# Weight splits in pieces during the scan, a partial first pass over four tiles of the output projection, and a partial first pass over three tiles of the last two down groups

## The reference

```
h      = modulate(rmsnorm(x, norm1_g))                 (and the same for the context)
q, k, v, o, gates, u, vb, ga, gb = split(h @ w_in)
h_a    = bidirectional chunked mLSTM scan(q, k, v, gates)      (4 heads, chunks of 128)
y_a    = rmsnorm(h_a, head_g) * sigmoid(o)
y_b    = gelu(u) * (w_spatial @ rmsnorm(gelu(vb)) + b)
merged = sigmoid(ga) * (y_a @ w_pa) + sigmoid(gb) * (y_b @ w_pb)
x      = x + g1 * (merged @ w_out)
f      = silu(h2 @ w_ff1) * (h2 @ w_ff3)               h2 = modulate(rmsnorm(x, norm2_g))
out    = rmsnorm(x + g2 * (f @ w_ff2), final_g)
```

## Time and profile before

| | us |
|---|---|
| median of 3 runs | 1909.56 (1909.21 to 1912.38) |
| the profiled execution | 1913.69 |
| its span | 1912.0 |
| PE busy / DVE busy / ACT busy | 1833.0 / 993.7 / 553.3 |

### The profile page before, as it was taken

The page is one execution under the profiler, slowest core; times in us unless marked ns, Lnnn a source line. Parts: engine busy times, 40 slices in busy tenths (PEclk is TensorE's granted clock), DMA queues, the critical chain, the costliest instruction groups (busy, mean ns, idle before and its releaser), DMA issues.

```text
span 1912.0 us, 24057 instructions
## 1 busy us (share of the span) xinstructions
PE 1833.0 (96%) x9052; PEld 1534.2 (80%) x9052; DVE 993.7 (52%) x1571; ACT 553.3 (29%) x842; POOL 131.8 (7%) x131
## 2 busy tenths in 40 slices
PE   6898999999989999999999999999999999999987
PEld 3596797978879988888888878788888888788876
DVE  3676636556355543211221164675655566666657
ACT  5533132322312322111221131443334333311111
POOL 1001010100112000000100000000000000231200
PEclk9899999999999899999999999999999999999989
DMA  7200100202048201111411152122222232632302
GB/s 295 60 17 17 56 23 23 66 22 66 12 137 282 88 22 44 57 53 44 124 52 44 44 176 88 66 66 67 93 82 88 66 100 76 232 130 89 122 8 88
DMA packets 91337, 157.15 MB, mean 82 GB/s; under 512 B 4466, under 2 KB 73218, under 8 KB 86930
## 3 DMA queue, kind: packets, MB, share of 16 engines
q1 hardware_dynamic: 83906, 130.11, 20.3%
q0 software_dynamic: 7376, 26.28, 4.1%
HBM read 132.26 MB, written 24.12 MB: 82 GB/s over the span
## 4 chain that ended last, share of the span: by engine, by line
PE 89%; DVE 7%; issue 2%; ACT 1%; DMA 0%; DVEq 0%; SPq 0%; ACTq 0%
PE PD L1803 26%; PE PD L1818 11%; PE PD L2164 10%; PE PM L2164 10%; PE PD L2183 6%; PE PM L2183 6%; PE PD L2090 5%; PE PM L1803 5%; PE PM L2108 1%; PE PD L2108 1%; PE PM L2038 1%; PE PD L1885 1%; DVE Cst L1382 1%; PE PM L1844 1%; PE PM L1876 1%
## 5 line engine op out<-in xcount | busy, mean ns | idle before, releaser
L1803 PE MATMUL PD<-R_hi,whi 128*128 128x512 f32 x480 | 149.8, 393 | 1.7 <-DVE Hh L1405 1.7
L1803 PE MATMUL PD<-R_lo,whi 128*128 128x512 f32 x480 | 148.5, 391 | 0.0
L1803 PE MATMUL PD<-R_hi,wlo 128*128 128x512 f32 x480 | 148.1, 390 | 0.0
L1818 PE MATMUL PD<-whi,R_hi 128*128 128x256 f32 x512 | 145.0, 283 | 0.0
L1818 PE MATMUL PD<-wlo,R_hi 128*128 128x256 f32 x512 | 144.9, 283 | 0.0
L1818 PE MATMUL PD<-whi,R_lo 128*128 128x256 f32 x512 | 144.9, 283 | 0.0
L1158 DVE TENSOR_TENSOR wlo<-raw,whi 128x1024 fp32r<-128x1024 f32 x76 | 89.9, 1219 | 93.7 <-ACT whi L745 93.7
L745 ACT ACTIVATE whi<-raw 128x1024 fp32r<-128x1024 f32 x76 | 76.4, 1049 | 158.9 <-PE PD L1803 95.5
L1803 PEld LDWEIGHTS PD<-R_hi,whi 128*128 128x128 f32 x480 | 89.2, 188 | 21.4 <-issue 3.0
L1803 PEld LDWEIGHTS PD<-R_hi,wlo 128*128 128x128 f32 x480 | 90.4, 188 | 19.2
L1803 PEld LDWEIGHTS PD<-R_lo,whi 128*128 128x128 f32 x480 | 90.4, 188 | 19.1
(11 more groups left out here) (406 smaller groups left out, 4097.7 us busy)
## 6 DMA issues: line engine op xcount, KB each, us to landing
raw<-in_w_in SPq DMA_DIRECT2D x46, 512.0 KB, 4.5
rawF<-in_w_ff SPq DMA_DIRECT2D x44, 512.0 KB, 5.0
ada<-in_w_ada POOLq DMA_DIRECT2D x32, 512.0 KB, 5.9
f_dram<-Fo SPq DMA_DIRECT2D x11, 1024.0 KB, 4.8
w_raw<-in_w_ff SPq DMA_DIRECT2D x11, 1024.0 KB, 5.0
f_raw<-f_dram SPq DMA_DIRECT2D x11, 1024.0 KB, 6.9
ada_raw<-in_w_ada SPq DMA_DIRECT2D x8, 1024.0 KB, 19.8
raw<-in_w_in SPq DMA_DIRECT2D x20, 256.0 KB, 3.6
```

Of the source, the lines that this page charges most:

```text
L1803: i = mm(dst[:, e * HALF:e * HALF + width], wk[:, k, :], part, start=(k == 0 and step == 0), stop=(k == KT - 1 and step == 2))
L1818: i = mm(PD[s][:, e * HALF:e * HALF + CW], src[:, k, at], wk[:, k, :], start=(k == 0 and step == 0), stop=(k == KT - 1 and step == 2))
```

## The change

Three edits, independent of one another.

1. Scan: the two halves of `wlo[A]`, made in j=3 and j=5, become eight pieces of 256 columns, one in each step from j=2 to j=9. `w_ready[0]` is counted after the piece of j=5 and `w_ready[1]` after that of j=9.
2. Output projection: ACT splits the second block of `w_out` after seven `m_hi`, and DVE after seven `m_lo`, both ahead of the last merge; `m_hi(7)` and `m_lo(7)` follow the merge. PE does k=0 to 6 of tiles 0 and 1, waits for the second PD buffer, does k=0 to 6 of tiles 2 and 3, then k=7 of the four tiles, then tiles 4 to 7 in full.
3. Down projection: PE does group 9's part of tiles 0 to 2 when group 9's split is there, then waits for group 10's split, does its part of these tiles, and then tiles 3 to 7 in full.

```diff
@@ ACT, gates_a
                 split_next(i * 2 + (N_PA + 2), A, None)
                 if last:
-                    for k in range(KT):
+                    for k in range(KT - 1):
                         m_hi(k)
                 split_next(i * 2 + (N_PA + 3), B, i * 2 + (T_PA + 2))
+                if last:
+                    m_hi(KT - 1)
@@ DVE
+            def split_lo_piece(n, buf, piece):
+
+                half, at = piece // 4, slice(piece * CW, (piece + 1) * CW)
+                dve.wait_ge(hi_done, n * 2 + (half + 1))
+                i = v.tensor_tensor(wlo[buf][:, at], raw[half][:, piece % 4 * CW:(piece % 4 + 1) * CW],
+                                    whi[buf][:, at].bitcast(F32), ALU.subtract)
+                if piece % 4 == 3:
+                    i.then_inc(w_ready[half], 1)
@@ DVE, attend
-                    if j in (3, 5):
-                        split_lo(h * 3 + (N_H + 3), A, (j // 2 - 1,))
+                    if j >= 2:
+                        split_lo_piece(h * 3 + (N_H + 3), A, j - 2)
                     if j < CT:
                         continue
@@ DVE, merge_a
                     if m == 0:
                         split_lo(i * 2 + (N_PA + 2), A)
                         if last:
-                            for k in range(KT - 2):
+                            for k in range(KT - 1):
                                 m_lo(k)
+                            split_lo(i * 2 + (N_PA + 3), B)
                 if last:
-                    for k in range(KT - 2, KT):
-                        m_lo(k)
-                split_lo(i * 2 + (N_PA + 3), B)
+                    m_lo(KT - 1)
+                else:
+                    split_lo(i * 2 + (N_PA + 3), B)
@@ PE
-            for m in range(2):
-                free(T_O + m)
-
-            def out_tile(hf, t):
+
+            def out_tile(hf, t, ks=range(KT)):
...
-                for k in range(KT):
+                for k in ks:
...
-                last.then_inc(out_mm, 1)
+                if ks[-1] == KT - 1:
+                    last.then_inc(out_mm, 1)
...
-            for t in range(LT):
+            free(T_O)
+            for t in range(2):
+                out_tile(0, t, range(KT - 1))
+            free(T_O + 1)
+            for t in range(2, 4):
+                out_tile(0, t, range(KT - 1))
+            for t in range(4):
+                out_tile(0, t, range(KT - 1, KT))
+            for t in range(4, LT):
                 out_tile(0, t)
...
-            def down(r, t, pars, halves_last=False):
-
-                pe.wait_ge(summed, r * LT + (t + 1))
+            def down(r, t, pars, halves_last=False, opens=True, closes=True):
+
+                if opens:
+                    pe.wait_ge(summed, r * LT + (t + 1))
...
-                              start=(n == 0), stop=(n == len(steps) - 1))
+                              start=(opens and n == 0), stop=(closes and n == len(steps) - 1))
...
-                    last.then_inc(down_done, 1)
+                    if closes:
+                        last.then_inc(down_done, 1)
...
+            pe.wait_ge(down_ready, 2 * NFB - 2)
+            for t in range(3):
+                down(NFB - 2, t, (1,), closes=False)
             pe.wait_ge(down_ready, 2 * NFB)
-            for t in range(LT):
+            for t in range(3):
+                down(NFB - 2, t, (0,), opens=False)
+            for t in range(3, LT):
                 down(NFB - 2, t, (1, 0), t == LT - 1)
```

## The result

The changed kernel takes 1899.44 us (median of 10 runs, 1898.38 to 1905.35), the kernel before 1909.61 in the same comparison (10 runs, 1906.77 to 1914.03). The ratio is 0.9949 with a 95% interval of 0.9939 to 0.9958, that is 9.7 us less (8.0 to 11.6). The forecast was 1900.8 within 1897.0 to 1906.5. The profiled execution took 1902.24, its span is 1899.7.

The account below looks back on a forecast made before the run. PE was taken as the bound, busy for 1833.0 of 1912.0 us. The terms 6.2 - 5.3 - 9.7 gave -8.8 us: 1904.9 for the profiled execution, 1900.8 for the median, range 1897.0 to 1906.5.

Parts of the forecast that it names:

- DVE's pieces: Scan, heads 0 to 2: six pieces, 2.04 us, replace 2.27 us before Hh's 14th write; 0.2 us gained per head, 0.6 together.
- One sign of the forecast: Scan: the changed profile would show DVE pieces of 0.42 us and no PE wait for `Cst`.
- The late load: Last head's scan: raw[1]'s later reload delays ACT's split and squares, 6.1 us slower, plus 0.7 us of low clock.
- the 6.2 of the forecast: Whole scan edit: -0.6 + 6.1 + 0.7 = 6.2 us slower, bounds 4.4 to 8.7.
- Heads 0 to 2 are covered: Scan, heads 0 to 2: the next head's first two matmul groups hide the delay; of 14 us cover, 8 remain.
- Output projection: Before the output projection: 3.6 us less wait and 1.7 us of clock, 5.3 us faster (3.1 to 5.3), 0.7 idle left.
- The join: Output projection, tiles 3 and 4: tile 0's residual ready at 1136.9, needed at 1137.3; a miss would cost under 0.5 us.
- Down projection: Last two down groups: no wait for group 10's split; 9.7 us faster, 3.0 of it clock (bounds 9.0 to 9.7).
- The free late load: Rival, scan's last head: the late load costs nothing, -15.5 us in all, 1894.1; chance 0.08.
- The output projection gives nothing: Rival: clock falls anyway and freed time becomes waits at k=7 or tile 4; -3.5 us in all, 1906.1; chance 0.11.
- The slow load: Rival, raw[1] in each head: late load uncovers all heads, kernel slower; break-even at 11.9 us load; chance 0.04.

Follow-up runs that it names:

- pieces early: The changed kernel with its eight pieces made two per step in j=2 to j=5, raw[1] given back in j=5: 1892.52 us, ratio 0.9915.
- two late halves: The changed kernel with two halves, in j=5 and j=9, instead of eight pieces: 1900.08 us, ratio 0.9945.
- squares first: The changed kernel with ACT's split of block B moved behind the eight squares, in every head: 1894.25 us, ratio 0.9914.
- the filled pause: The changed kernel with 56 unread PE products of 512 columns before the last head's transposes: 1901.35 us, ratio 0.9946.

## Why the prediction was right

**DVE's pieces.** Six pieces at 0.34 in place of 2.27 us: the next instruction starts 0.34 after a piece, as worked out from the 512 and 1024 columns of the earlier trace rows. Counted from head 0's transposes the last pause begins 1.0 us earlier; three times 0.2 was forecast. The sum of the waits for `Cst` and `Hh` fell by 0.7 (8.5 to 7.8). One sign of the forecast did not come: it had no wait of PE for `Cst`, and 5.4 us of them are left. They were 8 of up to 1.1 us and are 16 of 0.4 at most: smaller pieces shorten each of them and spread them over the steps. It has no weight in the sum, where they were counted at nothing. The Trainium skill, "VectorE: DVE Perf Modes", section on the TRN2 errata, gives an estimate of (256+151)/0.96 = 424 ns for a piece: the trace agrees with 0.42 as the length of one. Laid end to end such pieces would have made a loss; the trace has 0.08 of each overlapped by the next instruction, so the formula is right for the length of one and too dear for a row of them.

**The late load.** From the last piece to the end of the last square 9.5 us were forecast (538.2 to 547.7) and 9.45 measured (537.29 to 546.74). By parts: end of the piece to ACT's split 3.6 us (3.7), split 0.96 to the first square (1.06), squares 4.51 (4.3, as their spacing alternates between 0.53 and 0.62). PE's wait is 14.8 instead of 14.4, as PE is there a little earlier. The clock behind it loses 2.4 us instead of 1.6; 2.3 was taken. The scan edit measured so is +5.5 and +0.7, the 6.2 of the forecast (its upper bound of 8.7 doesn't follow from its terms, 0.8 + 6.1 + 1.4 = 8.3). By times it is +3.8 (the edit alone) and +6.7 (the whole change against the change without it), and the first of these is the worst-fitting number on the scan. Heads 0 to 2 are covered: no wait for their transposes appears. What PE waits for `Hh` there (2.4 us in 3) is for the 14th write, which was so before (1.7 in 3); with the waits for `Cst` shorter, PE comes to it sooner.

**Output projection.** 3.6 us of wait and 1.7 of clock: the stage is 5.3 shorter, with 0.68 us of idle left where 0.7 was forecast, and a clock of 1.00. The join has no wait.

**Down projection.** 243.4 us from first to last product were forecast (1647.2 to 1890.6), 243.3 measured (1644.70 to 1888.03). The stage began 2.5 us earlier, and tile 0 closes at 1855.9 for 1858.4, the next 2.65 us behind it. DVE falls behind and waits for PE again at 1877.58, at tile 5 rather than tile 6.

**The sum.** -8.8 was forecast, -10.2 is the difference of the medians (-9.7 by the ratio, -8.0 to -11.6 by its interval), -12.3 that of the spans. Of the last, 6.2 - 5.3 - 9.8 = -8.9 are the three edits, and 2.7 of the other 3.4 lie at 1228 to 1236, where nothing was changed. So the terms were right; most of what the single profile gave beyond them was the clock.

**The rivals.** The free late load fell with the kernel without the scan edit. "The output projection gives nothing" fell with the kernel that has it alone. The slow load did not occur: the longest of all 80 transfers of `raw` is 18.3 us in the change, but at this place 3.6 us pass from the end of the piece to ACT's split.

## What to carry to other kernels

When an instruction that gives a buffer back is moved later, follow the buffer: who loads it again, which engine takes up the load, and what stands behind that in the engine's order; the price was 6.2 us by the trace (3.8 and 6.7 by the times) for an edit that made DVE's own part 1.0 us shorter. A wait that only follows from another engine's length is worth nothing by itself (the scan's waits for `Cst` are 5.4 us with pieces late and 6.2 with pieces early, at the same ratio or better), so look for what is last there before cutting work into smaller pieces. And if a loop's last turn lacks the work that covers a step in the other turns, cost that turn by itself.

## What the runs showed of the hardware

**The spread of the runs goes with the granted clock.** The same kernel differs by some 7 us from run to run (the one before 1906.77 to 1914.03). Each run has its mean granted clock: in the kernel with two late halves the three runs with 0.978 have spans of 1903.1 to 1903.4 us, the four with 0.984 or 0.985 have 1894.8 to 1895.6. To see where it is lost, I cut the profiles into windows of 2 us and counted (1 - granted clock) x 2 us as the loss of each, at most half of PE's busy time in it. The sum is 26.1 us in the kernel before, 22.1 in the change, 16.8 with the two late halves. Many single losses are of 1.4 to 1.8 us, and those near 48, 144, 234 and 348 us stand in some profiles only.

Not all of them stand behind a pause. The largest is 5.1 us in nine of the twelve profiles and 6.8 in three. It lies between 636 and 664 us, where PE shows no idle time at all; PE does 64 products of a single column there, about 0.3 us long each. Timeline and window of the kernel before:

```profile
641.82 10.68 PE L2014 MATMUL PM<-one,Tacc 128*128 128x1 f32 x64
```

```profile
646.00:648.00 2.00, 2.00 (x11) 2.00 (x11) 0.04 (x1) 1.96 (x4) 0.00 (x0) 0.50 0.93 265
```

So a PE that the profile calls busy is not thereby a PE at the upper clock. No run here tested what lets it fall there.

Another place, the plain projection behind the output projection, has the same wait of 3.0 us for `R_lo` in all profiles. Windows behind it in the kernel before, then around it in the change:

```profile
1230.00:1235.00 5.00, 5.00 (x12) 3.94 (x13) 3.31 (x5) 2.25 (x4) 0.00 (x0) 0.50 0.00 0
```

```profile
1225.00:1230.00 5.00, 1.99 (x17) 1.51 (x15) 2.58 (x4) 3.49 (x7) 0.00 (x0) 1.00 0.54 187
1230.00:1235.00 5.00, 4.58 (x20) 3.86 (x21) 3.02 (x6) 2.73 (x5) 0.00 (x0) 1.00 0.00 0
```

In the first the clock was at 1.2 GHz for the whole stretch, and 2.8 us went. In the second it stayed at 2.4 GHz, after a stretch in which PE was busy for 1.99 of 5 us. In the kernel without the scan edit the loss here was 1.7 us. The forecast had treated the clock as given by the length of the wait. At the waits that the three edits touch this held in every profile here: low behind 4.3 us and more, high behind 0.7. At 3.0 us it did not, and what decides there stays open. For a reader it means that one profile's time can lie 4 us from the median of its kernel (1913.69 against 1909.61), while the lengths of stages, less their low-clock stretches, repeat far better. The part from head 0's transposes to the last product before the output projection takes 874.0 us in the kernel before and with the output edit alone, 874.2 without the scan edit and with the down edit alone, 873.7 with early pieces and with squares first; in the three kernels whose eight pieces are late and stand before the squares (the change, the scan edit alone, the filled pause) it takes 879.4, 879.7 and 879.5.
